# Gate and up products of two feed-forward layers as seven block products in place of eight

## The reference, cut to what matters

```python
def swiglu(h, w_gu, w_down):
    u = h @ w_gu
    g, v = u[..., :D_FF], u[..., D_FF:]
    return (jax.nn.silu(g) * v) @ w_down
...
h = h + swiglu(rmsnorm(h, norm_g[layer, 1]), ffn_w_gu[layer], ffn_w_down[layer])
```

## Time and profile before

| what | value |
|---|---|
| time, median of 3 runs | 2141.27 us (2141.06 to 2141.61) |
| span of the profiled execution | 2139.6 us, first to last instruction |
| its own time | not given apart from the span; the median of the runs lies 1.7 us above the span |
| TensorE (PE) busy | 98% of the span, 10474 matmuls |
| VectorE (DVE) busy | 59% |
| ScalarE (ACT) busy | 39% |
| GpSimd (POOL) busy | 13% |
| granted TensorE clock | 0.997 of full speed on average |
| 16 DMA engines, mean rate | 139 GB/s on average |

### The profile page before, as it was taken

How to read it: one execution, slowest core, us unless ns; L and a number is a source line. 1 busy time by engine, 2 the same in 40 slices (tenths; PEclk the granted TensorE clock), 3 DMA queues, 4 the chain that set the end, 5 groups by cost and what they waited for, 6 DMA issues and landing times.

```text
span 2139.6 us, 27223 instructions
## 1 busy us (share of the span) xinstructions
PE 2097.5 (98%) x10474; PEld 1579.8 (74%) x10474; DVE 1267.3 (59%) x1704; ACT 836.2 (39%) x1258; POOL 270.8 (13%) x234
## 2 busy tenths in 40 slices
PE   8999999999999999999999999999999999999998
PEld 6787788888878877888888888877778884333346
DVE  7887855554587678875655555488775454000038
ACT  6556522222253444774422222264542232222143
POOL 1334200000010064000100000020000023222220
PEclk9999999999999999999999999999999999999999
DMA  5322322223214352122322222212122158999961
GB/s 202 125 94 74 118 92 105 88 88 117 79 64 147 130 172 79 31 46 90 131 91 99 104 88 88 98 61 78 60 99 98 62 239 321 418 408 401 391 238 60
DMA packets 62622, 298.13 MB, mean 139 GB/s; under 512 B 14080, under 2 KB 14464, under 8 KB 34582
## 3 DMA queue, kind: packets, MB, share of 16 engines
q1 hardware_dynamic: 42560, 261.60, 32.0%
q0 software_dynamic: 19552, 34.55, 5.3%
q10 hardware_dynamic: 416, 0.70, 0.1%
HBM read 326.37 MB, written 22.48 MB: 163 GB/s over the span
## 4 chain that ended last, share of the span: by engine, by line
PE 80%; DVE 8%; DMA 5%; ACT 3%; issue 2%; POOL 1%; POOLq 0%; ACTq 0%; DVEq 0%
PE psum L652 21%; PE psum L654 21%; PE psum L653 21%; PE psum L1413 5%; PE psum L1437 3%; DMA panel<-w_m 3%; PE psum L1102 2%; PE psum L1077 1%; DVE a_lo L2137 1%; DMA over_panel<-w_m,over_row 1%; ACT a_hi L1520 1%; DVE xc L2294 1%; DVE hs L2248 1%; ACT hn_hi L1547 0%; PE psum L1235 0%
## 5 line engine op out<-in xcount | busy, mean ns | idle before, releaser
L652 PE MATMUL psum<-hn_hi,a_hi 128*128 128x512 f32 (+1 forms) x1592 | 628.2, 395 | 1.9 <-DVE a_lo L2126 0.9
L654 PE MATMUL psum<-hn_hi,a_lo 128*128 128x512 f32 (+1 forms) x1592 | 618.5, 389 | 0.0
L653 PE MATMUL psum<-hn_lo,a_hi 128*128 128x512 f32 (+1 forms) x1592 | 618.1, 388 | 0.0
L652 PEld LDWEIGHTS psum<-hn_hi,a_hi 128*128 128x128 f32 (+1 forms) x1592 | 297.0, 187 | 73.5 <-issue 7.8
L653 PEld LDWEIGHTS psum<-hn_lo,a_hi 128*128 128x128 f32 (+1 forms) x1592 | 297.1, 187 | 64.8 <-issue 2.4
L654 PEld LDWEIGHTS psum<-hn_hi,a_lo 128*128 128x128 f32 (+1 forms) x1592 | 297.0, 187 | 64.4
L2137 DVE TENSOR_TENSOR a_lo<-a_raw,a_hi 128x2048 fp32r<-128x2048 f32 (+2 forms) x108 | 247.2, 2289 | 69.6 <-ACT a_hi L1520 69.1
L1520 ACT ACTIVATE a_hi<-a_raw 128x2048 fp32r<-128x2048 f32 (+2 forms) x108 | 201.3, 1866 | 71.2 <-PE psum L654 62.0
L2236 DVE TENSOR_TENSOR h<-h,psum 128x512 f32<-128x512 f32 x176 | 119.4, 686 | 78.4 <-PE psum L654 78.4
L3150 POOL TENSOR_TENSOR sq<-sq 128x512 f32<-128x512 f32 x5 | 7.8, 1555 | 1118.2 <-ACT sq L1533 1118.2
L3072 DVE TENSOR_TENSOR xhid<-xsg,psum 128x256 f32<-128x256 f32 x24 | 10.1, 421 | 232.3 <-ACT xsg L2081 232.3
(11 more groups left out here) (533 smaller groups left out, 3261.2 us busy)
## 6 DMA issues: line engine op xcount, KB each, us to landing
a_raw<-w_a SPq DMA_DIRECT2D x115, 1024.0 KB, 5.0
panel<-w_m SPq DMA_DIRECT2D x96, 1024.0 KB
b_raw<-w_b SPq DMA_DIRECT2D x64, 512.0 KB, 3.4
q_scratch<-q_hi POOLq DMA_DIRECT2D x7, 384.0 KB
q_scratch<-qb_lo POOLq DMA_DIRECT2D x7, 384.0 KB
q_hi<-q_scratch POOLq DMA_DIRECT2D x7, 384.0 KB
q_lo<-q_scratch POOLq DMA_DIRECT2D x7, 384.0 KB
token_rows<-nat POOLq DMA_DIRECT2D x4, 512.0 KB, 5.5
```

The lines of the kernel that those rows point to most:

```text
L652: pe.matmul(out, w_hi, x_hi, start=first, stop=False)
L653: pe.matmul(out, w_hi, x_lo, start=False, stop=False)
L654: return pe.matmul(out, w_lo, x_hi, start=False, stop=last)
```

## The change

A feed-forward tile is a product of a 2 x 2 block matrix (rows: gate and up features; columns: the two halves of the contraction) with a 2 x 2 block matrix (the two halves of the contraction by two halves of 256 tokens). Before it costs eight block products, written as 48 matmuls of 512 tokens. Now tiles 2 to 21 of each layer take seven block products of 4 x 3 = 12 matmuls of 256 columns each (`seven`), 84 matmuls a tile, in the Strassen-Winograd form: P_1 and P_2 from plain blocks, P_3 from a block sum of the weights and plain tokens, P_4 from a plain block and a combination of tokens, P_5, P_6, P_7 from sums on both sides. Tiles 0 and 1 stay as they were.

- The sums of the weights, S_1 = A21 + A22, S_3, S_2 and S_4 (with signs already turned where needed) are made by four DMAs a tile that add into their target, 128 x 512 floats (256 KB) each, from SBUF to SBUF, issued by POOL (`sum_panel`). The first two are independent, the third waits for the first and for `low_1`, which reads the block that it overwrites, the fourth waits for the third. SP loads one quarter of each panel a second time, into `w_s3`, as the target of S_3.
- The token combinations are made once a layer: ACT writes the gained rows (`gain_x`, 8 of 512 columns), POOL makes four combinations of 256 columns for each of four contraction tiles (`make_tx`, 16 instructions), ACT and DVE split them.
- The split of a panel is now six pieces on ACT and DVE (`high_1`/`low_1` of 1024 columns, five of 512) into seven slots that lie over `a_hi` and `a_lo`; the slots are single, the raw panels still double.
- The products add onto each other in PSUM; between two of them ACT copies a partial sum out (`copy_1`, `copy_2`, `copy_3`, 256 columns) and DVE combines (`add_11`, `add_21`, `add_22`).
- P_3 and P_4 of a tile are run in the middle of the next tile's products, and the down products of a pair follow the first tile of the next pair.

```diff
+            def load_fast(a, b, q):
+                sp.wait_ge(hn_ready, KT * (q + 1))
+                with sp.Fori(1, FF_TILES // 2) as i:
+                    for v in range(2):
+                        load_a(a + v, i)
+                        sp.dma_start(w_s3[:, v, :, :].rearrange("p k n -> p (k n)"),
+                                     w_a[ds(a + v + 2 * i, 1), :, 2 * S:3 * S].rearrange("a p n -> p (a n)")) \
+                          .then_inc(s3_loaded[v], 16)
+                        load_b(b + v, i)
...
-            stream(A_FF0, B_FF0, FF_TILES // 2, 1)
+            load_fast(A_FF0, B_FF0, N_FFN0)
...
+            def seven(out, slot, x_hi, x_lo, again=False):
+
+                for k in range(KT // 2):
+                    mm = three(out, slot_hi[:, slot, k, :], slot_lo[:, slot, k, :], x_hi(k), x_lo(k),
+                               not again and k == 0, k == KT // 2 - 1, again)
+                return mm
+
+            def tx(n):
+                return lambda k: tx_hi[:, k, n, :], lambda k: tx_lo[:, k, n, :]
+
+            def hn_block(k0, c):
+                return lambda k: hn_hi[:, k0 + k, c], lambda k: hn_lo[:, k0 + k, c]
+
+            def fast_phase(sa, g, i, v):
+                n, m = sa + v + 2 * i, v - 2 + 2 * i
+                first = isinstance(i, int) and m == 0
+                x, z, y = bank[2 * v][:, 0:HALF], bank[2 * v + 1][:, 0:HALF], bank[2 * v + 1][:, HALF:S]
+                split, copied = split_at(g) + 5 * m, copied_at(g) + 3 * m
+                pe.wait_ge(tile_free, 2 * n - 2)
+                pe.wait_ge(w_split, split + 1)
+                seven(x, P_1, *hn_block(0, slice(0, HALF))).then_inc(w_used, 1)
+                seven(y, P_2, *hn_block(KT // 2, slice(0, HALF))).then_inc(w_used, 1)
+                if not first:
+                    pe.wait_ge(part_copied, copied)
+                    pe.wait_ge(w_split, split + 2)
+                    seven(bank[2 - 2 * v][:, 0:HALF], P_3, *hn_block(KT // 2, slice(HALF, S)), again=True) \
+                        .then_inc(w_used, 1)
+                else:
+                    pe.wait_ge(tx_ready, tx_at(g + 1))
+                pe.wait_ge(part_copied, copied + 1)
+                pe.wait_ge(w_split, split + 4)
+                seven(x, P_6, *tx(T2), again=True).then_inc(w_used, 2 if first else 1)
+                if not first:
+                    pe.wait_ge(a_ready, n)
+                    pe.wait_ge(part_added, added_at(g) + 2 * m)
+                    seven(bank[3 - 2 * v][:, 0:HALF], P_4, *tx(T4), again=True).then_inc(tile_ready, 2)
+                pe.wait_ge(part_added, added_at(g) + 2 * m + 1)
+                seven(z, P_7, *tx(T3)).then_inc(w_used, 1)
+                pe.wait_ge(part_copied, copied + 2)
+                pe.wait_ge(w_split, split + 5)
+                seven(x, P_5, *tx(T1), again=True).then_inc(w_used, 1)
+
+            def fast_last(sa, g):
+                pe.wait_ge(part_copied, copied_at(g + 1))
+                pe.wait_ge(w_split, split_at(g + 1))
+                seven(bank[2][:, 0:HALF], P_3, *hn_block(KT // 2, slice(HALF, S)), again=True).then_inc(w_used, 1)
+                pe.wait_ge(a_ready, sa + FF_TILES)
+                pe.wait_ge(part_added, added_at(g + 1))
+                seven(bank[3][:, 0:HALF], P_4, *tx(T4), again=True).then_inc(tile_ready, 2)
+
+            def ffn(sa, sb_, e, trips, q, t, g):
+                linear_first(sa, q, blocks=True)
                 sums(t)
-                linear(sa + 1)
+                linear(sa + 1, blocks=True)
+                fast_phase(sa, g, 1, 0)
                 down(sb_, e, 0, hid_hi, hid_lo, P)
-                with pe.Fori(1, trips) as i:
-                    linear(sa, i)
-                    linear(sa + 1, i)
-                    down(sb_, e, i, hid_hi, hid_lo, P)
-
...
+            def gain_x(k, gain):
+                for j in range(2):
+                    act.activation(x_of(k)[:, j, :], h[:, k + KT // 2 * j, :], ACT.Copy, scale=gain(k + KT // 2 * j)) \
+                       .then_inc(x_gained, 1)
+
+            def high_tx(g, k):
+                act.wait_ge(tx_made, tx_at(g, 4) + 4 * k + 4)
+                act.activation(tx_hi[:, k, :, :], tx_of(k), ACT.Copy).then_inc(tx_rounded, 1)
+
...
+            def high_s2(sa, g, i, v):
+                m = v - 2 + 2 * i
+                act.wait_ge(w_summed[v], summed_at(g) + 64 * i - 16)
+                if isinstance(i, int) and m == 0:
+                    act.wait_ge(tile_ready, 2 * sa + 2)
+                else:
+                    act.wait_ge(w_used, used_at(g) + 6 * (m - 1) + 4)
+                act.activation(slot_hi[:, P_6, :, :], part(v, S_2), ACT.Copy).then_inc(w_rounded, 1)
+
...
+            def first_pair(sa, sb_, e, t, g, gain):
+                gain_x(0, gain)
+                high_a(sa + 1)
+                for k in range(1, KT // 2):
+                    gain_x(k, gain)
+                high_tx(g, 0)
+                high_b(sb_)
+                high_tx(g, 1)
+                high_b(sb_ + 1)
+                high_tx(g, 2)
+                root_wide(t)
+                high_1(sa, g, 1, 0)
+                high_tx(g, 3)
+                silu(e, 0, 0)
+                high_hid(0, tile_free, 2 * sa + 2)
+                high_s3(sa, g, 1, 0)
+                high_s2(sa, g, 1, 0)
+                high_s1(sa, g, 1, 0)
+
+            def fast_pair(sa, sb_, e, i, g, last=False):
+                first = isinstance(i, int) and i == 1
+                copy_1(g, i, 0)
+                high_1(sa, g, i, 1)
+                high_s4(g, i, 0)
+                silu(e, i - 1, 1)
+                copy_2(sa, g, i, 0)
+                high_a22(sa, i, 0)
+                high_hid(1, *((tile_free, 2 * sa + 4) if first else (hid_made, hid_at(g) - 2 + 2 * i)))
+                high_s3(sa, g, i, 1)
+                high_s2(sa, g, i, 1)
+                copy_3(g, i, 0)
+                high_s1(sa, g, i, 1)
+                high_b(sb_, i)
+                copy_1(g, i, 1)
+                high_b(sb_ + 1, i)
+                if not last:
+                    high_1(sa, g, i + 1, 0)
+                high_s4(g, i, 1)
+                silu(e, i, 0)
+                copy_2(sa, g, i, 1)
+                high_a22(sa, i, 1)
+                high_hid(0, hid_made, hid_at(g) - 1 + 2 * i)
+                if not last:
+                    high_s3(sa, g, i + 1, 0)
+                    high_s2(sa, g, i + 1, 0)
+                copy_3(g, i, 1)
+                if not last:
+                    high_s1(sa, g, i + 1, 0)
+
...
+            def first_pair(sa, sb_, e, t, g):
+                low_a(sa + 1)
+                low_tx(g, 0)
+                low_b(sb_)
+                low_tx(g, 1)
+                low_b(sb_ + 1)
+                low_tx(g, 2)
+                inverse_wide(t)
+                gate(e, sa, 0, 0)
+                low_1(g, 0, 0)
+                low_tx(g, 3)
+                hidden(e, sa, 0)
+                low_hid(e, 0, 0)
+                low_s3(g, 0, 0, first=True)
+                low_s2(g, 0, 0)
+                gate(e, sa + 1, 0, 1)
+                low_s1(g, 0, 0)
+
+            def fast_pair(sa, sb_, e, i, g, last=False):
+                first = isinstance(i, int) and i == 1
+                n, m = sa + 2 * i, 2 * i - 2
+                add_11(g, m, 0)
+                scale_11(g, m, 0)
+                low_1(g, m + 1, 1)
+                if not first:
+                    scale_12(used_at(g) + 6 * m + 3, 1)
+                low_s4(split_at(g) + 5 * m + 7, 0)
+                if first:
+                    hidden(e, sa + 1, 1)
+                else:
+                    scale_gate(e, i - 1, 1)
+                    add_21(n - 1, 1)
+                    fast_hidden(e, n - 1, i - 1, 1)
+                low_a22(n, 0)
+                low_hid(e, i - 1, 1)
+                low_s3(g, m + 1, 1)
+                low_s2(g, m + 1, 1)
+                add_22(g, m, 0)
+                low_s1(g, m + 1, 1)
+                for k in range(4):
+                    add_y(sb_ - 2 + 2 * i, k)
+                low_b(sb_, i)
+                for k in range(4, KT):
+                    add_y(sb_ - 2 + 2 * i, k)
+                add_11(g, m + 1, 1)
+                scale_11(g, m + 1, 1)
+                low_b(sb_ + 1, i)
+                if not last:
+                    low_1(g, m + 2, 0)
+                scale_12(used_at(g) + 6 * m + 9, 0)
+                low_s4(split_at(g) + 5 * m + (11 if last else 12), 1)
+                scale_gate(e, i, 0)
+                add_21(n, 0)
+                fast_hidden(e, n, i, 0)
+                low_a22(n + 1, 1)
+                low_hid(e, i, 0)
+                if not last:
+                    low_s3(g, m + 2, 0)
+                    low_s2(g, m + 2, 0)
+                add_22(g, m + 1, 1)
+                if not last:
+                    low_s1(g, m + 2, 0)
+
+            def ffn(sa, sb_, e, trips, t, g):
+                first_pair(sa, sb_, e, t, g)
```

(41 more changed lines are left out.)

299 lines of the change are left out of this document (214 added, 85 removed).

## The result

After: 2307.36 us (median of 4 runs, 2306.43 to 2312.08); before, on the same chip, 2141.35. The ratio is 1.078, interval 1.0765 to 1.0795: 166 us slower where I had forecast 10 us faster. The profiled execution has a span of 2304.6 us at a mean clock of 0.970.

The account below looks back on a forecast made before the run. PE was taken to bound the kernel, so only the number and step of matmuls count. -32.0 + 11.7 + 4.4 + 6.2 = -9.7 us on a span of 2139.6, with the median 1.7 above the span: 2131.6 us, range 2116 to 2172.

Parts of the forecast that it names:

- The array's gain: Steady pairs on PE: fewer multiplications, at 0.120 us per 256-column matmul, save 1.60 us a pair, -32.0 us in all.
- rival 4: PE's 256-column matmuls step differently from 0.120 us when changing bank every 12; 0.01 us each is 34 us; chance 0.02.
- The refill of the odd panel: Mid down product, PE waits for additions queued behind the odd panel's late third sum: 0.6 to 0.7 us a pair, +11.7 us.
- rival 3: The adding DMA is the bound, stalling PE through DVE's queue, so the kernel is slower: 2158 or 2183 us; chance 0.40.
- A': Time from issue to landing of the second of two adding DMAs running side by side, taken as 3.7 us.
- A: Time from issue to landing of one 256 KB adding DMA, taken as 3.2 us, from 3.1 to 5.5.
- Z: Moment the odd panel's S_2 is in place, 6.1 + A' + A; it may be 12.4 before PE waits.
- S: PE's stand per pair in the down product, max(0, A' + A - 6.3): 0.6 to 0.7 us; bounds 0 and +92 us overall.
- PE meets nothing late: Second tile of a steady pair: walking its operations in order, no hand-over to PE comes late, so no cost.
- the prediction's own signs of being wrong: PE waiting at P_6 or P_5 for a split, DVE idle over 1 us before additions, step above 0.125, or late POOL.
- Entry: Start of each layer: late root and POOL's combinations delay PE by 2.2 us a layer, +4.4; bounds 0 and 6 a layer.
- Exit: End of each layer: PE stands 3.1 us behind the next stage's panel split, +6.2 us for both; bounds 0 and 8.

Follow-up runs that it names:

- e1: Kernel after, but SP holds the even panel's load until the odd panel's third sum has landed, from the third pair on; 2226.04 us, ratio 1.0401.
- e4: Kernel after with each adding DMA cut to one of four contraction tiles, 64 KB, the other sums left out; 2168.71 us, ratio 1.0133.
- e5: Kernel after with additions first, plus silu and copy_2 ahead of high_1 and S_4 on ACT, DVE reordered likewise; 2152.3 us, ratio 1.0054.
- e6: Kernel after with additions first, plus each layer's entry and exit reordered on ACT, DVE and POOL; 2182.9 us, ratio 1.0193.

## Why the prediction was wrong

**The array's gain: right.** 0.12 us a step over the changes of bank; rival 4 falls. The accounting above closes with -32.0.

**The refill of the odd panel: the step that failed.** The prediction had the right place, releaser and queue (PE's wait in the middle of the down product behind `low_s2`, `add_22`, `low_s1`), rival 3's mechanism, and a wrong size. With t = 0 at 430.70, the start of the pair's first tile, the panel's load is issued at -0.2 (said: -0.3). The first two sums go out at 7.6 and 8.1, not 5.4 and 6.0: +2.1. Beside the panel and its extra quarter two things were in flight that I had not priced, the 512 KB of `b`, issued 0.5 us behind, and the even panel's fourth sum; how the 2.1 us divide between them no run shows. From the second sum's issue to the third's it is 4.6 us, where I had A' = 3.7: +0.9. The third takes 8.1, not A = 3.2: +4.9. Less 0.1 for a hand-over, Z is 20.8 in place of 13.0. From Z to the end of the first addition it is 2.9 us (said: 3.1). PE itself comes there at 17.5 and not 15.5, for its wait at P_5, so that it stands 6.2 us here. In the first layer the additions' waits average 6.0 us (53.6 / 9), where I had S = 0.65; with the second layer it is 4.7 (89.9 / 19).

The data to see it stood in my own working: "it is freed near t = 10" of the even panel, and 6.0 + A' = 9.7 for the issue of the third sum. I laid two transfers on the same moment and priced one as if alone. A = 3.2 itself was right: ACT starts on the sum 3.3 us behind its issue where no load is beside it (e1). By rows of that size alone I also let the bound end at 5.5, where two transfers in flight together needed the time of both. So what would be late was said, and how late was not: S at 4.0 + 4.4, rival 3's own price, gave 2158, and even its bound of +92 us counted no lower clock and no second wait. My range ended at 2172, although rival 3 also priced 2183 and the bound lay far beyond it. Two slips changed nothing: at A' + A = 7.7 a pair loses 1.4 us, not yet the 1.6 that the array saves, and DVE has eight operations of 512 a tile besides `low_1` and `low_b`, not seven, with which the sum of 12.8 us comes out.

**The page Collectives: The Full Stack of the Trainium skill (the bandwidth ceiling)**, by which a reducing DMA is held back by its two reads, gave an estimate of 4.7. By itself a sum took 3.3 to 3.6, so the estimate was too high here. The 8.1 us beside a load are no support for it either: they go when the load is moved (e1), and with a quarter of the bytes it is still 6.1 to 6.5 (e4).

**"PE meets nothing late" up to P_5: wrong**, 35.5 us in 18 waits. Walking ACT's queue I had left out that `high_1` waits for the panel's load and `high_s4` for a fourth sum that runs beside the loads of 430.48; both stand ahead of `silu` and `copy_2`. e5 shows by order alone that it is this queue. Of the prediction's own signs of being wrong two had come, this one and DVE idle for 7.45 us ahead of the additions.

**The clock: a term that the prediction put at nothing.** Each wait of some 6 us was followed by slower steps, 1.8 to 2.4 us a time in the first layer; of the 201 us of excess 50.8 are steps without a wait.

**Entry: too small**, 6.15 and 9.55 us of wait, where I had 2.2 a layer. ACT, then DVE, in the kernel after:

```profile
265.91 0.67 ACT L1679 ACTIVATE rn<-psum,cn 128x512 f32<-128x512 f32 x1
```

```profile
267.31 3.34 DVE L2423 RECIPROCAL rn<-rn 128x512 f32<-128x512 f32 x1
...
274.34 0.69 DVE L2660 TENSOR_TENSOR hid<-sg,psum 128x512 f32<-128x512 f32 x1
```

The root comes at 265.9, not 260.5: it stands behind `high_tx(2)`, which waits for POOL, and I had given POOL 0.75 us a combination where it took up to 2.67. The bound of 6 was passed, by the queue and not by POOL alone (e6). **Exit: right**, 2.0 and 3.4 us of wait and copy for 3.1 each, 6.0 in the accounting for 6.2.

## What to carry to other kernels

When a change adds transfers, write down every transfer in flight with its issue and landing, and price two that go out together by their bytes together; a row of one alone is only the lower bound. Moments count: a sum beside a load that went out with it took 6.9 to 8.4 us, and one that went out 1 us ahead of the load hardly more than alone. In an in-order queue put what the bounding engine waits for ahead of what waits for a DMA: here that order was worth more (119 us) than making the DMA punctual (81), and with it punctuality was worth nothing measurable. And a release that moves on one engine moves the loads behind it.
